# A two-layer flow backbone on one core: closings by groups of feature blocks, and layer 0's conditioning in products of 512 columns

## The chip, the cores and the metric

One core of a Trainium2 chip (trn2) runs the kernel once per launch. The metric is the device time of one execution in microseconds; a smaller number is better. The times shown are medians of several executions, and one execution more is profiled.

## What is computed

Two token groups pass through the same two layers: 128 context tokens and 256 latent (sample) tokens of 2048 features, 384 tokens in all. Each group has one conditioning vector, from which a layer makes six modulation vectors (shift, scale and gate, twice). In the reference, cut to what matters here:

```python
def trunk_layer(x, cvec, ctx_kv, lp):
    mods = jnp.split(jax.nn.silu(cvec) @ lp['w_ada'] + lp['b_ada'], 6, axis=-1)   # w_ada: 2048 x 12288
    sh1, sc1, g1, sh2, sc2, g2 = [m[:, None, :] for m in mods]
    h = rms_norm(x, lp['g_pre1']) * (1.0 + sc1) + sh1
    z = h @ lp['w_in']                                    # 2048 x 3072: q, k, v, pool, conv
    ...                                                   # attn (16 heads), pool, conv
    mix = jnp.concatenate([attn, pool, conv], axis=-1) @ lp['w_out']
    x = x + g1 * rms_norm(mix, lp['g_post1'])
    h = rms_norm(x, lp['g_pre2']) * (1.0 + sc2) + sh2
    f = jnp.square(jax.nn.relu(h @ lp['w_mlp1'])) @ lp['w_mlp2']   # 2048 x 8192 x 2048
    x = x + g2 * rms_norm(f, lp['g_post2'])
    return x, kv_out
```

All of it is float32.

## The kernel before

**Weights.** They stream from memory once, in loads of 512 KB into four slots (`raw`). ACT makes a high part of each load (`w_high`, L602), VectorE the low part that is left (`w_low`, L902), and TensorE multiplies three times (high by high, high by low, low by high) with the same split of the activations (`h_hi`, `h_lo`). Such a load is a *unit*; four units are a *quad*. `unit` (L1482) has 24 products of 384 columns; `unit_all` and `unit_tok` (L1491) keep the tokens still and stream 512 weight columns. ACT makes unit n + 4's high part when TensorE has used unit n, and SP loads a slot when its low part is made, so the four units ahead of TensorE are split and up to four behind those are loaded.

**Order.** Every engine's program is written out by hand, with semaphores between them. SP issues all streaming loads in one order. Layer 0 begins with eight 512-column blocks of `w_ada` that bring the first shift and scale. Then, in each layer: projections in pairs of blocks (`two_blocks`, eight units each); the attention loop (`step`, 24 steps: scores, softmax, turn, mix) with the first half of the output projection in pieces between (`side_piece`); the second half of the output projection and a *closing*; the MLP in eight chunks of eight quads; and again a closing, but for the last layer.

**Layer 0's conditioning.** The other 24 blocks of 256 columns of layer 0's `w_ada` (the gate of the first part, shift and scale of the second) run beside the projections (10 blocks) and the attention loop (14). A block is four quads of products in the four column groups of TensorE (`ada_unit`, L1565), each for one load of 512 rows by 256 columns. Its four partial rows are copied out by VectorE (`ada_copy`, L907), turned and added by TensorE (`ada_turn`, L1574), and added to the bias by VectorE (`ada_mods`, L911). A block's first product waits for the mods of the block before it.

**The later conditioning.** Layer 0's last gate and layer 1's blocks, 28 of 512 columns, are multiplied by VectorE during the MLPs (`products`, L933), up to three blocks in a chunk, two quads each. Such a block is folded by a transpose (L938) and a reduction (L942) into spare columns of `cond`, and TensorE turns it (`turn_sums`, L1616, four small products). That is done for each block, in the quads 2, 5 and 7. One late block runs in layer 1's projections.

**A closing** (`close_stage` on PE, ACT and VectorE, then `turn_x`). The last quarter of the output is added and gated for each token tile (tile 0 context, tiles 1 and 2 sample), its squares are summed, a Sqrt on ACT (`root_f`, L658) and a reciprocal give the norm, and x is updated (`update_x`, L1003). The squares of the new x give the next norm as a diagonal (`norm_x`, L1021). `turn_x` (L1546) multiplies 16 blocks of x of a tile by the diagonal, which turns and scales them at once. Then scale and shift are applied from PSUM (`modulate`: ACT L677, VectorE L1028, each four times 128 columns), and the result is split (`norm_high` L684; low parts by POOL, L510, for tiles 0 and 1 and by VectorE, L1036, for tile 2). The tiles go one after another, and fillers (`keep_warm`, L1535) stand after a tile's turns. Behind the last low part POOL zeroes the MLP's accumulator (L593), for which VectorE waits ahead of its MLP loop. The first unit of the next stage needs feature group 0 of all tiles (`h_wait`).

Of the kernel before, what the change touches and what calls it, by code (L numbers as in the profile page):

```python
# [31 lines left out]
F32 = mybir.dt.float32  # L32
# [5 lines left out]
P = 128  # L38
# [35 lines left out]
MODS_END = (ADA_BLOCKS, ADA_BLOCKS + ADA_WIDE)  # L74
# [6 lines left out]
WIDE_TURNS = (2, 5, 7)  # L81
WIDE_BLOCKS = ({0: ((0, 20, 1), (1, 0, 2), (1, 1, 2)), 4: ((1, 8, 3), (1, 9, 3), (1, 10, 3))},
# [8 lines left out]
def turn_of_quad(layer, lo, blocks=3):  # L91

    return {WIDE_TURNS[s]: s for s in range(min(blocks, len(WIDE_BLOCKS[layer][lo])))}

# [17 lines left out]
ADA_FIRST = (7, 6)  # L112
X_BANKS = (4, 5)
PAIRS = 8
ADA_FIRST_BLOCKS = 8
# [3 lines left out]
TURN_BANKS = ((4, 5, 6, 3), (0, 1, 2, 4), (5, 6, 3, 4))  # L119
TURN_FREED = ((None, None, None, None), (None, None, None, (0, 0)), ((0, 1), (0, 2), (0, 3), (1, 3)))  # L120
FILL = (0, 1, 5)
# [11 lines left out]
ADA_STEPS = 3 * (ADA_BLOCKS - ADA_MIX) // 2  # L133

# [34 lines left out]
def backbone(nc, x_prompt, x_sample, cache_k, cache_v, c, c_ctx, w_ada, b_ada, g_pre1, g_post1, g_pre2,  # L169
# [3 lines left out]
    with ctx:  # L173
# [44 lines left out]
        cond = new("cond", [DT, 32])  # L218
        folded = cond[:, :, 2:4].rearrange("p n g -> p g n")
# [4 lines left out]
        ada_s = at("ada_s", [UC], F32, sums_at + 4 * TOK)  # L224
# [6 lines left out]
        sinks = new("sinks", [DEPTH, HEADS])  # L231
# [49 lines left out]
        inv_x = at("inv_x", [TT], F32, stats_at + 288)  # L281

# [19 lines left out]
        xt_ready, full_act, full_dve, norm_hi, norm_lo, early_lo = sems("xt_ready full_act full_dve norm_hi norm_lo early_lo")  # L302
# [39 lines left out]

        block = ctx.enter_context(nc.Block())
# [3 lines left out]
        def _(sp):  # L347
# [35 lines left out]
            def load_blocks(layer, w, q, col, ada):  # L383

                for j in range(8):
                    load_unit(j, q, part(w, layer, 512 * (j % 4), col + UC * (j // 4)))
                    if ada is not None:
                        load_ada(ada[0], ada[1] + j // 4, j % 4)
# [20 lines left out]
            for layer in range(DEPTH):  # L409
# [20 lines left out]
                def load_pair(i, half, j, m):  # L430

                    for k in range(4):
                        load_ada(0, m, k)
                    load_out(i, half, j)
                    for k in range(2):
                        load_ada(0, m + 1, k)
                    load_out(i, half, j + 1)
                    for k in range(2, 4):
                        load_ada(0, m + 1, k)
# [49 lines left out]
        def _(pool):  # L489
# [3 lines left out]
            nc.gpsimd.memset(cond[:, :, :], 0.0).then_inc(consts_ready, 1)  # L493
# [9 lines left out]
            def early_lows(p):  # L503

                for t in range(2):
                    for g in range(4):
                        kts = slice(4 * g, 4 * g + 4)
                        pool.wait_ge(gate_done, 12 * p)
                        pool.wait_ge(norm_hi, 12 * (p - 1) + 4 * t + g + 1)
                        nc.gpsimd.tensor_tensor(h_lo[:, kts, tokens(t)], full[:, kts, tokens(t)], h_hi[:, kts, tokens(t)].bitcast(F32),  # L510
                                                ALU.subtract).then_inc(early_lo, 1)

            for layer in range(DEPTH):
                if layer == 0:
                    pool.wait_ge(h_ready, 8)
                else:
                    early_lows(2 * layer)
                    pool.wait_ge(early_lo, 8 * 2 * layer)
# [71 lines left out]
                early_lows(2 * layer + 1)  # L590
                pool.wait_ge(early_lo, 8 * (2 * layer + 1))
# [5 lines left out]
        def _(act):  # L597
# [74 lines left out]
            def modulate(p, t, g, layer, k, shift):  # L672

                act.wait_ge(xt_ready, 12 * (p - 1) + 4 * t + g + 1)
                for i in range(4):
                    kt = 4 * g + i
# [1277 lines left out]
```

## Time and profile before

| | us |
|---|---|
| median of 3 runs | 3249.17 |
| lowest and highest | 3248.01, 3249.87 |
| the profiled execution, whole | 3251.47 |
| its span, from the first to the last instruction | 3249.7 |
| TensorE busy in it | 3157.3 (97%) |
| VectorE, ACT, POOL busy | 2151.5, 1111.1, 215.8 |
| mean granted clock of TensorE | 0.99 of full |

The page gives busy time by engine, a chain of work that ended last, and groups of instructions by line. Busy shares are means over stages with different limits, so the stages are read one by one: with the table of stretches and the order of time. A float32 product stands as two records.

### The profile page before, as it was taken

To read this page: it belongs to the slowest core of one execution; us is meant where nothing else is said; L and a number is where in the kernel's file an instruction comes from. 1 tells how busy PE (TensorE), PEld (TensorE's weight loads), DVE (VectorE), ACT (ScalarE), POOL (GpSimd) and SP (SyncE) were. 2 spreads that over 40 slices of the span, in tenths; PEclk is the share of its full clock that TensorE was granted. 3 is DMA by queue.
4 is the path that set the end of the run, shared out by engine and by line. 5 is a ranking of instruction groups with operands and counts; after the bars stand their busy time and mean duration, and the time that the engine had idled before them with its cause. 6 is when DMAs were issued, how large, how long until landed. Compare 5 with 4: busy or idle time off the path is not lost.

```text
span 3249.7 us, 46901 instructions
## 1 busy us (share of the span) xinstructions
PE 3157.3 (97%) x16999; PEld 2733.6 (84%) x16999; DVE 2151.5 (66%) x3087; ACT 1111.1 (34%) x1531; POOL 215.8 (7%) x235
## 2 busy tenths in 40 slices
PE   7999999999999999999999999999999999999999
PEld 2688656798898998989988996679989899898997
DVE  2366665698988989889876888666646553334335
ACT  2222333533332333323334334353333233332333
POOL 0020132200000000000001303320000000000000
PEclk9999999999999999999999999999999999999999
DMA  9865575367676666767664331234545544444443
GB/s 350 285 208 185 164 233 175 128 218 228 217 222 217 225 218 208 229 212 237 208 213 134 111 124 61 95 119 156 175 132 178 167 138 128 130 126 126 129 124 142
DMA packets 404975, 574.75 MB, mean 177 GB/s; under 512 B 17881, under 2 KB 243921, under 8 KB 403441
## 3 DMA queue, kind: packets, MB, share of 16 engines
q1 hardware_dynamic: 401216, 560.02, 53.3%
q10 hardware_dynamic: 2288, 8.78, 0.7%
q0 software_dynamic: 1344, 4.33, 0.4%
q8 instruction: 72, 1.18, 0.1%
q14 instruction: 55, 0.44, 0.0%
HBM read 569.32 MB, written 3.74 MB: 176 GB/s over the span
## 4 chain that ended last, share of the span: by engine, by line
PE 86%; DVE 6%; issue 3%; ACT 2%; DMA 2%; SPq 0%; DVEq 0%; ACTq 0%
PE ps L1482 42%; PE ps L1491 35%; PE ps L1565 2%; DMA ada_raw<-in_w_ada_dram 1%; DVE w_lo L902 1%; DVE ada_sums L933 1%; PE ps L1588 1%; PE ps L1659 1%; PE ps L1750 1%; DVE conv L1191 1%; PE ps L1776 1%; PE ps L1764 1%; PE ps L1737 1%; ACT full L677 1%; DVE x L1003 1%
## 5 line engine op out<-in xcount | busy, mean ns | idle before, releaser
L902 DVE TENSOR_TENSOR w_lo<-raw,w_hi 128x1024 fp32r<-128x1024 f32 x660 | 810.0, 1232 | 737.2 <-ACT w_hi L602 716.1
L602 ACT ACTIVATE w_hi<-raw 128x1024 fp32r<-128x1024 f32 x660 | 697.8, 1059 | 1454.5 <-PE ps L1491 757.8
L1482 PE MATMUL ps<-h_hi,w_hi 128*128 128x384 f32 x2752 | 929.0, 338 | 4.9 <-DVE h_lo L1036 3.9
L1482 PE MATMUL ps<-h_hi,w_lo 128*128 128x384 f32 x2752 | 922.2, 335 | 0.0
L1482 PE MATMUL ps<-h_lo,w_hi 128*128 128x384 f32 x2752 | 921.9, 335 | 0.0
L1491 PE MATMUL ps<-w_hi,hid_hi 128*128 128x512 f32 x1500 | 586.0, 391 | 2.6 <-DVE facc L1404 2.6
L1491 PE MATMUL ps<-w_hi,hid_lo 128*128 128x512 f32 x1500 | 584.0, 389 | 0.0
L1491 PE MATMUL ps<-w_lo,hid_hi 128*128 128x512 f32 x1500 | 584.0, 389 | 0.0
L933 DVE SCALAR_TENSOR_TENSOR ada_sums<-ada_raw,cond,ada_sums 128x512 f32<-128x512 f32 x840 | 574.8, 744 | 0.0
L1482 PEld LDWEIGHTS ps<-h_hi,w_hi 128*128 128x128 f32 x2752 | 518.5, 188 | 21.2 <-issue 18.5
L1482 PEld LDWEIGHTS ps<-h_lo,w_hi 128*128 128x128 f32 x2752 | 518.4, 188 | 1.1
L1482 PEld LDWEIGHTS ps<-h_hi,w_lo 128*128 128x128 f32 x2752 | 518.2, 188 | 0.0
L1491 PEld LDWEIGHTS ps<-w_hi,hid_hi 128*128 128x128 f32 x1500 | 281.6, 188 | 63.3 <-DVE facc L1404 5.5
L1491 PEld LDWEIGHTS ps<-w_lo,hid_hi 128*128 128x128 f32 x1500 | 281.6, 188 | 58.6
L1491 PEld LDWEIGHTS ps<-w_hi,hid_lo 128*128 128x128 f32 x1500 | 281.6, 188 | 57.5
L1491 PE MATMUL ps<-w_hi,h_hi 128*128 128x512 f32 x348 | 149.0, 428 | 0.0
L1191 DVE SCALAR_TENSOR_TENSOR conv<-glu,pc,conv 128x384 f32<-128x384 f32 x240 | 141.8, 652 | 0.0
L1491 PE MATMUL ps<-w_lo,h_hi 128*128 128x512 f32 x348 | 138.4, 398 | 0.0
L1491 PE MATMUL ps<-w_hi,h_lo 128*128 128x512 f32 x348 | 138.4, 398 | 0.0
L1404 DVE TENSOR_TENSOR facc<-facc,ps 128x512 f32<-128x512 f32 x168 | 115.0, 685 | 30.4 <-PE ps L1491 28.5
L858 ACT ACTIVATE z<-ps 128x768 f32<-128x768 f32 x64 | 52.2, 815 | 202.8 <-PE ps L1482 202.8
L510 POOL TENSOR_TENSOR h_lo<-full,h_hi 128x512 fp32r<-128x512 f32 x24 | 34.3, 1466 | 1211.6 <-ACT h_hi L684 1211.6
(226 smaller groups left out, 2176.9 us busy)
## 6 DMA issues: line engine op xcount, KB each, us to landing
raw<-in_w_mlp_dram SPq DMA_DIRECT2D x512, 512.0 KB, 3.9
ada_raw<-in_w_ada_dram SPq DMA_DIRECT2D x360, 512.0 KB, 4.6
raw<-in_w_in_dram SPq DMA_DIRECT2D x96, 512.0 KB, 4.8
raw<-in_w_out_dram SPq DMA_DIRECT2D x64, 512.0 KB, 3.7
ada_aside<-in_w_ada_dram SPq DMA_DIRECT2D x24, 512.0 KB, 10.5
out_dram<-x SPq DMA_DIRECT2D x6, 512.0 KB, 2.6
x<-in_x_sample_dram SPq DMA_DIRECT2D x1, 2048.0 KB, 9.9
pw_w<-in_w_conv_pw_dram POOLq DMA_DIRECT2D x2, 1024.0 KB, 7.0
```

What stands on the lines that cost most here:

```text
L510: nc.gpsimd.tensor_tensor(h_lo[:, kts, tokens(t)], full[:, kts, tokens(t)], h_hi[:, kts, tokens(t)].bitcast(F32), ALU.subtract).then_inc(e ...
L602: nc.scalar.activation(dst[:, j % 4, :, :], raw[:, j % 4, :, :], ACT.Copy).then_inc(hi_ready, 1)
L677: last = nc.scalar.activation(full[:, kt, tokens(t)], ps[:, TURN_BANKS[t][g], P * i:P * i + P], ACT.Identity, scale=coef[:, k, kt, group(t ...
L858: nc.scalar.activation(z[:, 16:18, :], ps[:, 2 * pair:2 * pair + 2, 0:TOK], ACT.Relu).then_inc(acc_free, 1)
L902: nc.vector.tensor_tensor(low[:, j % 4, :, :], raw[:, j % 4, :, :], high[:, j % 4, :, :].bitcast(F32), ALU.subtract).then_inc(lo_ready, 1)
L933: op = nc.vector.scalar_tensor_tensor(out=out, in0=src, scalar=by, in1=out, op0=ALU.mult, op1=ALU.add)
L1003: nc.vector.scalar_tensor_tensor(out=res, in0=src, scalar=inv_f[:, t:t + 1], in1=res, op0=ALU.mult, op1=ALU.add).then_inc(x_updated, 1)
L1191: op = nc.vector.scalar_tensor_tensor(out=out, in0=src, scalar=w, in1=out, op0=ALU.mult, op1=ALU.add)
L1404: nc.vector.tensor_tensor(dst, dst, ps[:, BANK_ACC + t, :], ALU.add).then_inc(acc_added, 1)
L1482: last = nc.tensor.matmul(ps[:, 2 * pair + t, 0:TOK], w[:, j % 4, k, P * t:P * t + P], v[:, kt + k, :], start=begin and k == 0 and i == 0, ...
L1491: last = nc.tensor.matmul(ps[:, bank + t, :], v[:, kt + k, tokens(t)], wide(w, j)[:, k, :], start=begin and k == 0 and i == 0, stop=end an ...
L1565: last = nc.tensor.matmul(ps[32 * g:32 * g + 32, BANK_ADA, 0:UC], cond[:, 4 * j + g, :], ada_raw[:, j, g, :], start=j == 0, stop=j == 3)
```

## The change

- **Conditioning of layer 0.** The 24 blocks of 256 columns become 12 of 512, loaded as 256 rows by 512 columns. `ada_pair` multiplies two loads in one go, four products of 512 columns in the four column groups, behind every second unit and at four places in three attention steps. The blocks aren't turned one by one: `cond_at(kt, slot)` shifts the two vectors inside the 32 stationary columns, so that each block of a batch adds into rows of its own of the same bank, over a margin of zeros. There are two batches, of four and of eight blocks; each has one `batch_copy`, one `batch_turn` and one `batch_mods`. TensorE's loop over three pairs of projection blocks is written out in layer 0.
- **Closings.** The context tile is turned first. Then the sample tiles stand side by side in PSUM, and groups of four feature blocks are turned, modulated in 256 columns, split and freed one after another; POOL makes the context's low parts only, VectorE the sample's. ACT runs one Sqrt on a constant ahead of the closing (`root_seed`), and modulates a first context group before the last tile's squares. The fillers are one and four.
- **Turns of block sums.** `turn_sums` runs once for each chunk of an MLP, for its one to three blocks together.
- The sinks are kept once, with their sign changed.

```diff
-            def load_ada(layer, m, j):
-                sp.wait_ge(ada_used, 4 * m + j - 3)
-                src = w_ada[layer, 512 * j:512 * j + 512, bass.ds(m * UC, UC)]
-                sp.dma_start(ada_raw[:, j, :, :], src.rearrange("(k p) n -> p k n", p=P)).then_inc(ada_landed[j], 16)
+            def load_ada(layer, m, half, j):
+                sp.wait_ge(ada_used, 4 * m + (4 * half + j - 3))
+                row = 4 * 2 * P * half + 2 * P * j
+                src = w_ada[layer, row:row + 2 * P, bass.ds(m * UC, NC)]
+                sp.dma_start(wide(ada_raw, j), src.rearrange("(k p) n -> p k n", p=P)).then_inc(ada_landed[j], 16)
...
+            def ada_pair(w, v):
+                batch = 0 if w < BATCHES[1][0] else 1
+                first, n = BATCHES[batch]
+                begin, end = w == first and v == 0, w == first + n - 1 and v == 3
+                for u in (2 * v, 2 * v + 1):
+                    pe.wait_ge(ada_landed[u % 4], 16 * (2 * w + u // 4 + 1 - ADA_ASIDE))
...
+                for u in (2 * v, 2 * v + 1):
+                    for k in range(2):
+                        g = 2 * (u % 2) + k
+                        last = nc.tensor.matmul(ps[32 * g:32 * g + 32, BANK_ADA, :], cond_at(2 * u + k, w - first),
+                                                wide(ada_raw, u)[:, k, :], start=begin, stop=end)
+                    last.then_inc(ada_used, 1)
...
-                    if ada is not None:
-                        ada_beside(ada, j)
+                    if ada is not None and j % 2:
+                        ada_pair(ada, j // 2)
...
             def turn_x(p):
-                for t in range(TT):
-                    for g in range(4):
-                        pe.wait_ge(xn_ready, 3 * (p - 1) + t + 1)
...
+                pe.wait_ge(xn_ready, 3 * (p - 1) + 1)
+                for g in range(4):
+                    for i in range(4):
+                        last = turn_block(0, 4 * g + i, CTX_BANKS[g], P * i)
+                    last.then_inc(xt_ready, 1)
...
+                keep_warm(FILL[0], BANK_ADA)
+                pe.wait_ge(xn_ready, 3 * (p - 1) + 2)
+                turn_lat(1, 0)
+                keep_warm(FILL[1], BANK_ADA)
+                pe.wait_ge(xn_ready, 3 * (p - 1) + 3)
+                turn_lat(2, 0).then_inc(xt_ready, 1)
+                for g in range(1, 4):
+                    if g > 1:
+                        pe.wait_ge(full_act, ctx_full(p, 2 * g - 4))
+                        pe.wait_ge(full_dve, ctx_full(p, 2 * g - 3))
+                    turn_lat(1, g)
+                    turn_lat(2, g).then_inc(xt_ready, 1)
...
             def close_stage(r, before, layer, k, shift, q):          # VectorE
...
-                modulate(p, 0, 1, layer, k, shift)
+                modulate_ctx(p, 1, *how)
                 sum_squares_x(r, 2)
-                modulate(p, 0, 3, layer, k, shift)
                 norm_x(p, 2)
-                modulate(p, 1, 1, layer, k, shift)
-                modulate(p, 1, 3, layer, k, shift)
+                modulate_ctx(p, 3, *how)
+                modulate_lat(p, 0, *how)
+                low_lat(p, 0)
+                modulate_lat(p, 1, *how)
                 w_low(3, q)
-                modulate(p, 2, 1, layer, k, shift)
-                norm_low(p, 2, 0)
-                modulate(p, 2, 3, layer, k, shift)
-                for g in range(1, 4):
-                    norm_low(p, 2, g)
+                low_lat(p, 1)
+                for g in (2, 3):
+                    modulate_lat(p, g, *how)
+                    low_lat(p, g)
...
             def close_stage(r, q, layer, k, shift):                  # ACT
...
+                nc.scalar.activation(root_seed[:, :], ones[:, 0:1], ACT.Sqrt)
                 square_f(r, 3, 0)
                 root_f(r, 0)
...
-                        if k in turns and j == 2:
-                            turn_sums(wide_before(layer, lo, i, turns[k]))
+                        if k == turn_quad(layer, lo, blocks) and j == 2:
+                            turn_sums(wide_before(layer, lo, i, 0), blocks_of_chunk(layer, lo, blocks))
```

## Rows read from the trace of the kernel before

**Rows 1.** The page: TensorE's busy time, its share of the span, and its instructions.

```profile
PE 3157.3 (97%) x16999; PEld 2733.6 (84%) x16999; DVE 2151.5 (66%) x3087; ACT 1111.1 (34%) x1531; POOL 215.8 (7%) x235
```

**Rows 2.** Table of stretches: length, PE, PEld, DVE, ACT, POOL busy (count), clock, DMA, GB/s.

```profile
137.70:380.80 243.10, 231.35 (x1412) 197.57 (x1412) 156.88 (x236) 66.16 (x71) 26.83 (x41) 0.98 0.55 177
380.80:533.00 152.20, 148.29 (x1123) 90.12 (x1124) 89.05 (x223) 49.97 (x153) 45.99 (x40) 0.98 0.74 235
1732.50:1799.30 66.80, 66.78 (x384) 66.51 (x384) 42.07 (x53) 20.02 (x23) 4.13 (x8) 1.00 0.53 163
1732.50:1967.10 234.60, 227.66 (x1252) 217.51 (x1252) 188.33 (x265) 76.14 (x84) 34.18 (x52) 0.99 0.41 126
1967.10:2074.50 107.40, 103.89 (x619) 72.71 (x620) 82.56 (x195) 49.53 (x153) 45.86 (x40) 1.00 0.20 64
```

**Rows 3.** Order of time, layer 1's late turn: start, length, what, [idle before it, releaser].

```profile
1802.78 0.25 PE L1616 MATMUL ps<-cond,fold 128*32 128x8 f32 x8 [3.43 <-DVE cond L942]
```

**Rows 4.** Groups of PE by line: busy, mean ns of a record, idle before, releaser.

```profile
L1565 PE MATMUL ps<-ada_raw,cond 128*32 128x256 f32 x768 | 59.9, 394 | 7.9 <-DVE mods L911 7.9
L1574 PE MATMUL ps<-fold,ada_s 128*128 128x2 f32 x96 | 13.2, 242 | 7.8 <-DVE ada_s L907 7.8
```

**Rows 5.** Order of time, PE: two quads after a unit, then one quad.

```profile
141.77 0.34 PE L1482 MATMUL ps<-h_hi,w_lo 128*128 128x384 f32 x1
142.04 1.07 PE L1565 MATMUL ps<-ada_raw,cond 128*32 128x256 f32 x16
...
143.32 0.34 PE L1482 MATMUL ps<-h_lo,w_hi 128*128 128x384 f32 x1
...
147.14 0.34 PE L1482 MATMUL ps<-h_hi,w_lo 128*128 128x384 f32 x1
...
148.26 0.34 PE L1482 MATMUL ps<-h_lo,w_hi 128*128 128x384 f32 x1
```

**Rows 6.** DMA: size and median us to landing; attention loop of layer 0, then start.

```profile
ada_raw<-in_w_ada_dram SPq DMA_DIRECT2D x50, 512.0 KB, 4.9
raw<-in_w_out_dram SPq DMA_DIRECT2D x16, 512.0 KB, 6.3
...
ada_raw<-in_w_ada_dram SPq DMA_DIRECT2D x18, 512.0 KB, 10.0
```

**Rows 7.** Order of time: layer 0's closing behind attention, to VectorE's first MLP unit.

```profile
611.12 1.28 ACT L658 ACT_TABLE_LOAD   x1
612.65 0.16 DVE L998 RECIPROCAL inv_f<-std_f 128x1 f32<-128x1 f32 x1 [1.17 <-ACT std_f L658]
618.34 3.73 PE L1546 MATMUL ps<-diag,x 128*128 128x128 f32 x32
625.28 0.74 DVE L1003 SCALAR_TENSOR_TENSOR x<-gated,inv_f,x 128x512 f32<-128x512 f32 x1
625.95 1.36 DVE L1028 TENSOR_SCALAR full<-ps,coef,mods 128x128 f32<-128x128 f32 x4
628.97 0.29 DVE L1021 TENSOR_SCALAR diag<-ident,inv_x 128x128 f32<-128x128 f32 x1
641.03 0.43 PE L1482 MATMUL ps<-h_hi,w_hi 128*128 128x384 f32 x1 [0.76 <-DVE h_lo L1036]
650.53 1.23 DVE L902 TENSOR_TENSOR w_lo<-raw,w_hi 128x1024 fp32r<-128x1024 f32 x1 [5.63 <-POOL facc L593]
```

**Rows 8.** Order of time, VectorE in the first MLP chunk: one unit's four products.

```profile
658.71 2.73 DVE L933 SCALAR_TENSOR_TENSOR ada_sums<-ada_raw,cond,ada_sums 128x512 f32<-128x512 f32 x4
```

**Rows 9.** Table of stretches (columns as rows 2): first low parts of both MLPs.

```profile
650.50:719.90 69.40, 69.40 (x391) 67.07 (x391) 68.16 (x89) 26.82 (x29) 0.00 (x0) 1.00 0.67 212
2192.10:2228.70 36.60, 36.60 (x213) 36.60 (x212) 34.06 (x44) 14.37 (x15) 0.00 (x0) 1.00 0.56 173
```

**Rows 10.** Order of time, PE: the products around one turn of block sums.

```profile
686.72 0.34 PE L1482 MATMUL ps<-h_hi,w_lo 128*128 128x384 f32 x1
...
687.45 0.34 PE L1482 MATMUL ps<-h_lo,w_hi 128*128 128x384 f32 x1
```

More of the change, by code:

```diff
@@ L133 @@
 ADA_STEPS = 3 * (ADA_BLOCKS - ADA_MIX) // 2
+ROW_CHUNKS = (256, 384, 512, 896)
 def taps_at(u):
@@ L675, in modulate, with modulate_ctx @@
+            def modulate_ctx(p, g, *how):
+                act.wait_ge(xt_ready, ctx_turned(p, g))
                 for i in range(4):
-                    kt = 4 * g + i
-                    last = nc.scalar.activation(full[:, kt, tokens(t)], ps[:, TURN_BANKS[t][g], P * i:P * i + P], ACT.Identity,
-                                                scale=coef[:, k, kt, group(t):group(t) + 1],
-                                                bias=mods[:, layer, shift + kt, group(t):group(t) + 1])
+                    last = modulate(4 * g + i, 0, CTX, ps[:, CTX_BANKS[g], P * i:P * i + P], *how)
@@ L966, in eight_units @@
                         f()
-            def ada_pair(layer, m):
-                n = layer * ADA_BLOCKS + m
-                return ({3: [lambda: ada_copy(n)], 4: [lambda: ada_mods(layer, m, n)], 7: [lambda: ada_copy(n + 1)]},
-                        {7: [lambda: ada_mods(layer, m + 1, n + 1)]})
             def add_f(r, n, t, before):
@@ L1199, in _ @@
                 for i in range(3):
-                    before, after = ada_pair(0, i * 2 + ADA_QKV) if first else ({}, {})
-                    for j in range(8):
-                        after[j] = [lambda c=c: tap(c) for c in taps_at(8 * i + j)] + list(after.get(j, []))
-                    eight_units(quad(layer, Q_IN + 4) + i * 2, before, after)
+                    after = {j: [lambda c=c: tap(c) for c in taps_at(8 * i + j)] for j in range(8)}
+                    eight_units(quad(layer, Q_IN + 4) + i * 2, None, after)
                 def pool_means():
@@ L1341, in _ @@
                     what = i % 3
-                    m = ADA_MIX + 2 * (i // 3)
-                    if first and what == 0 and 0 < i <= ADA_STEPS:
-                        ada_mods(0, m - 1, m - 1)
-                    if first and what == 1 and i < ADA_STEPS:
-                        ada_copy(m)
                     if i >= 4:
@@ L1576, in ada_turn, with batch_turn @@
+            def batch_turn(batch):
+                n = BATCHES[batch][1]
+                pe.wait_ge(ada_copied, 2 * ADA_FIRST_BLOCKS + batch + 1)
+                for t in range(4):
+                    last = nc.tensor.matmul(ps[:, BATCH_BANKS[batch], 2 * n * t:2 * n * t + 2 * n],
+                                            sums_flat[:, ROW_CHUNKS[t]:ROW_CHUNKS[t] + P], fold[:, 0:2 * n], start=True, stop=True)
                 last.then_inc(ada_turned, 1)
@@ L1816, in step @@
                         if ada and what == 0:
-                            ada_unit(m, 3)
-                        if ada and what == 1:
-                            ada_unit(m + 1, 0)
-                        if ada and what == 2:
-                            ada_turn(m + 1)
+                            ada_pair(w, 1)
                     if i >= 3:
```

358 lines of the change are left out of this document (193 added, 165 removed).

## Prediction

> **What bounds the kernel now.** The page comes first: TensorE is busy for 3157.3 of 3249.7 us [rows 1], so a gain has to come from work taken off TensorE's queue or from the 92 us in which it stands. The table of stretches shows where the two layers differ, and that is the yardstick here: layer 1 runs the same projections and the same attention loop as layer 0, without layer 0's conditioning products between them [rows 2]. Attention with its side units takes 152.2 us in layer 0 and 107.4 us in layer 1. The stretch from the first whole pair of projection blocks to the first scores takes 243.1 us with 40 units in layer 0, and 234.6 us with 48 units in layer 1. Sixteen undisturbed units take 66.8 us, so one takes 4.175 us and one of its 24 products 0.174 us. Layer 1's 234.6 us hold one late block turn, which stood 3.43 us [rows 3] and costs 0.4 us itself.
>
> **Layer 0's conditioning.** 24 blocks of 256 columns become 12 of 512. Before, TensorE turns aside once for each quad of `ada_unit` (four products in four column groups) and once for each `ada_turn`; the groups by line give 768 and 96 records, and 7.9 us of waiting for VectorE's `ada_mods` and 7.8 us for its `ada_copy` [rows 4]. The price of one aside comes from the order of time: from the last product before a single quad to the second product after it are 1.12 us, two product steps (0.35 us) of which would have passed anyway, so it costs 0.77 us; two quads in one place cost 1.55 - 0.35 = 1.20 us [rows 5]. So a quad streams for 0.43 us, and turning aside costs 0.34 us. Twice the columns make 0.86 us for a quad of 512 columns; the streaming stays the same in sum, and the asides halve.
>
> Projections: layer 1's 234.6 us less the late turn (3.8) and eight units (33.4) leave 197.4 us as the bare stretch; layer 0 pays 45.7 us on top for ten blocks. After the change these are five wide blocks, 20 asides of 0.86 + 0.34 us, 24.0 us, and one batch turn of four small products, not in the trace: 0.4 us if it is like a turn of block sums (below), 1.2 if its full-width weights count three times; I take 0.8, nearer to the former. Together 24.8 us. **Gain 20.9 us.** Layer 1's stretch contains its own waits for VectorE's tail (layer norm, pooling); if layer 0 meets less of them, up to 2 us more.
>
> Attention: 152.2 - 107.4 = 44.8 us for 14 blocks. 56 quads stream 24.1 us, 14 turns at 0.38 us make 5.3 us, and the granted clock of 0.98 on 152 us costs 3.0 us; what is left is 12.4 us, 0.22 us for each aside (some of them stand where TensorE changes operands anyway). After: 28 asides of 0.86 + 0.22, 30.2 us, and 0.8 us for the second batch turn. With 0.34 us an aside it would be 34.4 us. Gain 10.4 to 13.8 us, from which I take 1.4 us for a DMA wait (next paragraph): **12.4 us.** The waits for VectorE's copies and mods [rows 4] are inside both differences; the batch's own copy stands in VectorE's queue ahead of a low part, with three units ready for TensorE behind it, so it hides.
>
> What is moved is the wait on the loads. `ada_pair` needs two loads at once and frees two at once, and SP, which issues in order, holds the weight loads behind the conditioning loads: in the projections four of eight weight loads are now issued four units ahead of their use instead of five or six. Three units are 13 us; a load lands in 4.9 to 6.3 us in the busiest stretch [rows 6], and the splits into high and low parts take ACT and VectorE some 2.3 us; so it stays covered by 4 us, and that is what goes first if the loads slow down. In the attention loop the third pair of a block is loaded when the first is used, a step and a pair before (107.4 / 24 + 1.1 = 5.6 us), where a load's median is 4.9 to 6.3 us. Between nothing and 0.7 us for each of seven blocks, I take 0.2, as a pair is only of the 4.9 us kind.
>
> **The closings** (three). TensorE's part runs from the end of VectorE's residual update U to the first unit of the next stage: U = 625.28 + 0.74 = 626.0 and the unit at 641.0, 15.0 us [rows 7]; the same pair of rows stands in all three closings, 15.0 us each. Behind U, before: two modulations (1.36 us each) and the norm, so the third diagonal at U + 3.2; 16 turns, five fillers, the tail of ACT's modulations and splits. After: one modulation and the square of the last tile on ACT, diagonal at about U + 2.7; then 28 turns at 3.73 / 16 = 0.233 us without a wait, to U + 9.4. The first unit needs only feature group 0, whose split I have done at U + 7.5. That chain is turn, two 256-column modulations, a 1024-column split on ACT and one on VectorE; the modulation is not in the trace, it lies between one and two of 128 columns (0.34 to 0.68 us), and I take 0.48, nearer to one since an operation of 512 columns takes 2.73 / 4 = 0.68 us [rows 8] and not four times 0.34; the ends move the unit by nothing, since TensorE's turns end last. So the unit starts at U + 9.5, **5.5 us earlier, three times**. ACT and VectorE go on with groups 1 to 3 until about U + 20, one unit ahead of TensorE.
>
> The early Sqrt takes a function-table load out of the chain in the two closings behind attention. The load is 1.28 us, and VectorE waited 1.17 us for the root [rows 7]; from the load's end to the reciprocal are 0.25 us, which stay with a handover, 0.3 in all: 0.87 us each, 1.7 us for both. The Trainium skill, page "ScalarE: Activation LUTs", section "What ACT_TABLE_LOAD costs", counts a drain of 1.38 us on top of a load of 1.283 us. The trace agrees on the load; the square root ran right behind it, so no row shows that drain. By the skill's figures it would be an estimated 5.3 us for two and the time 3.6 us lower.
>
> Not all of it stays. VectorE starts the MLP's low parts only when POOL has zeroed the accumulator, at 650.5 us [rows 7], and that clock hardly moves, since the zeroing waits for the last low part. TensorE stood 6 us behind VectorE there; with a start at 634.7 its unit 4 is due at 651.4 and VectorE has it at 651.7. From there VectorE needs 68.2 us of work for 16 units in layer 0, and 34.1 us for eight in layer 1, whose products end there [rows 9]; TensorE needs 66.4 (the last four units have 18 products of 512 columns, some 4.1 us) and 33.4. With the 0.3 us that is **2.0 us back** in layer 0 and, counted in the same way, **0.8 us back** in layer 1. The middle closing leads into projections with few products and keeps all. Closings: 16.5 + 1.7 - 2.8 = **15.4 us**.
>
> **Turns of block sums in the MLP.** 28 become 13 (23 in layer 0 become 8). One costs 0.73 - 0.35 = 0.38 us [rows 10]; fifteen are 5.7 us. 24 columns instead of 8 in eight of them return some 0.4 us: **5.3 us**. The last turn of each chunk stays where it was, so its wait doesn't change; two more small `block_mods` at the end of a chunk fall into VectorE's idle quad.
>
> The merged sinks, the zeroed margin of the conditioning vectors and SP's wider rows cost nothing: they lie at the start beside loads, or change no count.
>
> **Sum:** 20.9 + 12.4 + 15.4 + 5.3 = 54.0 us. The profiled execution took 3251.5 us (span 3249.7 and 1.8 around it), so 3197.5; it lies 2.3 us over the median of the three runs, so the forecast is **3195 us**. Bounds: projections 16 to 23, attention 6 to 17, closings 8 to 19, turns 4 to 6.
>
> **Rivals.**
> (a) VectorE takes the closings back: if the tail of a closing on ACT and VectorE is 3 us longer than I have it, the MLP starts 3 us later in both layers and unit 1 waits too; the closings keep 5 us and the time is 3205. For it: VectorE is the only engine with work in that hole, and 650.5 is a wait for POOL. Against it: VectorE's own work there stays some 11 us (28 instructions become 20), and POOL has four low parts left instead of eight.
> (b) The loads become the wait: with pairs freed at once the mean landing grows to 8 us; the third and fourth pair of each attention block wait some 1.5 us each and three of eight weight units 0.5 us, 27 us in all: 3222. For it: that loop already has DMA at 0.74 [rows 2], and a shorter loop raises it to 0.82. Against it: rows are 2 KB instead of 1 KB, and no wait for this load shows before.
> (c) The four column groups don't run side by side at 512 columns: a quad would cost 1.72 us, 48 times 0.86 us more: 3236. Against it: two 256-column quads in one place add 0.43 us, what four groups side by side make.
> (d) Slower. The attention loop becomes bound by the latency of its pairs: TensorE stands at each of its 28 pairs, with the softmax chain behind it on the same queue. It decides at 54 / 28 = 1.9 us a pair; at 2.5 us the time is 3265. For that a load would have to land in 8 us and more on all pairs; it took 10.0 us where the queues were full in the start [rows 6], but here 4.9.
>
> **How the numbers follow.** Forecast 0.74, (a) 0.11, (b) 0.09, (c) 0.03, (d) 0.03. The forecast's own bounds give 3184 to 3215 with all terms at one end, which is unlikely; the range 3182 to 3214 takes in (a) and a quarter of (b), and 2 us below for the spread of the runs shown. 0.2% is 6.5 us, about what a measurement of this kernel can tell from no change. The forecast, (a), (b) and (c) are all faster, 0.97; of (d) I put 0.01 within 0.2% (1.9 us a pair) and 0.02 beyond it.
>
> **What would show it.** In the profile after: records of the conditioning products in the same stretches at half the count and some 0.6 us each, quads of 1.0 us; no idle time of TensorE in front of them on VectorE; 222 and 138 us for the two stretches of layer 0; first unit 9 to 10 us behind U in each closing, and no table load in the chain; then waits for `w_lo` in the first MLP chunk of layer 0, some 2 us; 104 records of block sums, eight a turn [rows 3], instead of 224. It is wrong if TensorE waits for `ada_raw`, if weight units wait for ACT's high parts in the projections, or if the first chunk of the MLP ends at the time at which it ended before.

## The result and the profile after

| | before | after |
|---|---|---|
| median, us | 3249.5 | 3217.5 |
| profiled execution, us | 3251.5 | 3218.1 |
| its span, us | 3249.7 | 3215.7 |
| ratio to before | | 0.990 [0.989, 0.991] |

The change makes the kernel 32 us faster; the forecast was 54 us, 3195 us, with a range that ended at 3214. The page of after, to be held against [rows 1]:

```profile
span 3215.7 us, 45526 instructions
...
PE 3126.3 (97%) x16409; PEld 2707.3 (84%) x16409; DVE 2149.1 (67%) x3021; ACT 1104.2 (34%) x1498; POOL 204.6 (6%) x223
```

TensorE's busy time fell by 31.0 us. The table of stretches shows where the forecast's 54 us came and where they did not. Columns as in [rows 2]; in order of time: layer 0's projections, its attention loop, the first closing from the first turn to the first unit, the first MLP chunk, the second chunk; the middle closing, which leads into layer 1; then the last closing and the first chunk of layer 1's MLP.

```profile
138.04:368.38 230.34, 220.73 (x1220) 188.57 (x1221) 153.94 (x219) 65.66 (x71) 30.75 (x41) 0.99 0.57 187
368.38:507.30 138.92, 135.68 (x847) 75.91 (x846) 84.58 (x197) 49.52 (x153) 45.92 (x40) 1.00 0.76 258
592.69:609.01 16.32, 15.19 (x107) 12.45 (x106) 13.61 (x32) 13.08 (x29) 2.98 (x2) 1.00 0.48 162
609.01:751.13 142.12, 136.34 (x683) 122.36 (x682) 123.45 (x156) 48.62 (x53) 8.72 (x3) 0.98 0.61 195
751.13:884.11 132.98, 132.69 (x682) 120.57 (x680) 118.19 (x153) 43.60 (x44) 0.00 (x0) 1.00 0.68 221
1682.06:1698.41 16.35, 15.20 (x108) 12.45 (x106) 13.63 (x32) 13.08 (x29) 2.99 (x2) 1.00 0.01 2
2126.63:2142.95 16.32, 15.20 (x108) 12.45 (x106) 13.61 (x32) 13.09 (x29) 2.98 (x2) 1.00 0.48 162
2142.95:2282.45 139.50, 134.60 (x683) 122.38 (x682) 78.69 (x89) 48.58 (x53) 8.72 (x3) 0.99 0.45 144
```

The closings and first chunks of the kernel before, in the same view and order (22.69 us of closing and 133.84 of chunk in layer 0, the middle closing 21.78, 22.69 and 133.79 in layer 1):

```profile
618.34:641.03 22.69, 18.17 (x110) 14.07 (x108) 16.43 (x43) 19.30 (x47) 9.33 (x7) 0.92 0.49 163
641.03:774.87 133.84, 133.47 (x696) 120.92 (x697) 120.01 (x157) 44.50 (x48) 7.37 (x3) 1.00 0.61 198
1710.74:1732.52 21.78, 18.15 (x110) 14.21 (x108) 15.52 (x43) 19.29 (x47) 9.29 (x7) 0.92 0.08 25
2159.96:2182.65 22.69, 16.50 (x109) 12.96 (x108) 16.34 (x43) 19.29 (x47) 9.32 (x7) 0.99 0.50 163
2182.65:2316.44 133.79, 133.79 (x680) 122.27 (x681) 75.09 (x88) 44.47 (x48) 7.36 (x3) 0.99 0.45 142
```

By stretch, in us gained (the spans differ by 34.0; the measured column adds up to that but for rounding):

| stretch | forecast | measured |
|---|---|---|
| projections of layer 0 | 20.9 | 12.8 |
| attention loop of layer 0 | 12.4 | 13.3 |
| three closings, first turn to first unit | 18.2 | 6.4 + 5.4 + 6.4 = 18.2 |
| what the first MLP chunks give back | -2.8 | -9.1 - 5.7 = -14.8 |
| turns of block sums | 5.3 | 0.8 + 4.9 = 5.7 |
| the start, and layer 1's projections and attention | 0 | -0.3 - 2.0 + 1.2 = -1.1 |

(The first chunk of layer 0 is 8.3 us longer and saves 0.8 of turns like every chunk there; so it gives back 9.1.) Two rows are wrong: 12 us in the first chunks and 8 us in the projections.

**The first MLP chunk.** Order of time in layer 0: the start, the length, what, and in brackets the idle time before it and its releaser. First VectorE, then TensorE, then one stretch of the table with the granted clock third from the end:

```profile
626.09 1.23 DVE L959 TENSOR_TENSOR w_lo<-raw,w_hi 128x1024 fp32r<-128x1024 f32 x1 [5.62 <-POOL facc L632]
...
694.42 3.48 DVE L959 TENSOR_TENSOR w_lo<-raw,w_hi 128x1024 fp32r<-128x1024 f32 x3
697.82 2.12 DVE L1466 TENSOR_TENSOR facc<-facc,ps 128x512 f32<-128x512 f32 x3
```

```profile
698.56 0.79 PE L1553 MATMUL ps<-w_hi,hid_hi 128*128 128x512 f32 x1 [3.69 <-DVE facc L1466]
699.15 0.63 PE L1553 MATMUL ps<-w_hi,hid_lo 128*128 128x512 f32 x1
699.58 0.63 PE L1553 MATMUL ps<-w_lo,hid_hi 128*128 128x512 f32 x1
...
704.34 0.39 PE L1553 MATMUL ps<-w_lo,hid_hi 128*128 128x512 f32 x1
704.57 0.39 PE L1553 MATMUL ps<-w_hi,hid_hi 128*128 128x512 f32 x1
```

```profile
698.56:703.56 5.00, 5.00 (x12) 3.94 (x13) 2.49 (x3) 0.00 (x0) 0.00 (x0) 0.50 0.97 338
```

VectorE begins the MLP at 626.09 us, as in [rows 7] held up by POOL's zeroing, and comes to its first add at 697.82 without a pause. TensorE stands 3.69 us for that add. Then the granted clock is 0.50 for 5 us (1.2 of 2.4 GHz): twelve products step by 0.43 us, where they step by 0.23 at 704 us, 2.6 us more. In layer 1 the same lag shows at the turn of block sums (behind this hole the granted clock is 0.66 on the mean of 5 us):

```profile
2194.45 0.25 PE L1692 MATMUL ps<-cond_all,fold 128*32 128x8 f32 x8 [3.75 <-DVE cond_all L1005]
```

**The projections.** Here TensorE stands twice, 4.08 us for the batch's copy and 3.66 us for the conv taps that the sums of the layer norm need. SP, ACT and VectorE ahead of the first, VectorE ahead of the second, then both products:

```profile
290.89 0.37 SPq L405 DMA_DIRECT2D ada_raw<-in_w_ada_dram  x1
291.44 1.13 SPq L391 DMA_DIRECT2D raw<-in_w_in_dram  x1
```

```profile
297.57 1.06 ACT L641 ACTIVATE w_hi<-raw 128x1024 fp32r<-128x1024 f32 x1 [5.95 <-DMA raw<-in_w_in_dram]
```

```profile
298.67 1.23 DVE L959 TENSOR_TENSOR w_lo<-raw,w_hi 128x1024 fp32r<-128x1024 f32 x1 [3.66 <-ACT w_hi L641]
299.81 2.73 DVE L1258 SCALAR_TENSOR_TENSOR conv<-glu,pc,conv 128x384 f32<-128x384 f32 x5
...
302.92 0.28 DVE L968 COPY sums_flat<-ps 128x128 f32<-128x128 f32 x1
...
311.27 1.23 DVE L959 TENSOR_TENSOR w_lo<-raw,w_hi 128x1024 fp32r<-128x1024 f32 x1 [4.29 <-ACT w_hi L641]
312.41 2.20 DVE L1258 SCALAR_TENSOR_TENSOR conv<-glu,pc,conv 128x384 f32<-128x384 f32 x4
```

```profile
303.35 1.07 PE L1650 MATMUL ps<-ada_raw,cond_all 128*32 128x512 f32 x8 [4.08 <-DVE sums_flat L968]
314.80 4.51 PE L1780 MATMUL ps<-conv,ones 128*128 128x384 f32 x8 [3.66 <-DVE small L1264]
```

SP issues the weight load only behind the conditioning load whose slot comes free with the pair at 290.7 us; it lands 6 us later; ACT's high part, the low part, five taps and only then the copy follow. The second hole has the same shape: a low part that waits 4.29 us for its high part, and four taps behind it. How the waiting is shared between the two holes changes from execution to execution: in three other runs that leave the projections as they are (the old closings, the moved wait and the run without zeroing below) they are 3.9 and 4.1, 2.7 and 4.7, and 2.6 and 4.8 us, 7.4 to 8.0 together.

### The profile page after: what moved, and what is told of

It is laid out like the page before. It is cut to its first block, busy times and chain, and to the rows that moved or that the text cites. A ratio compares the mean times of both kernels' runs of the same rounds, so it can differ in the third digit from the quotient of the medians.

```text
span 3215.7 us, 45526 instructions
## 1 busy us (share of the span) xinstructions
PE 3126.3 (97%) x16409; PEld 2707.3 (84%) x16409; DVE 2149.1 (67%) x3021; ACT 1104.2 (34%) x1498; POOL 204.6 (6%) x223
## 4 chain that ended last, share of the span: by engine, by line
PE 82%; DVE 8%; issue 5%; DMA 3%; ACT 2%; POOL 0%; SPq 0%; DVEq 0%; ACTq 0%; POOLq 0%
PE ps L1544 40%; PE ps L1553 35%; DVE ada_sums L996 2%; DMA ada_raw<-in_w_ada_dram 2%; DVE w_lo L959 1%; PE ps L1650 1%; PE ps L1673 1%; PE ps L1735 1%; PE ps L1861 1%; PE ps L1849 1%; PE ps L1835 1%; PE ps L1822 1%; DVE x L1061 1%; DMA raw<-in_w_in_dram 0%; ACT w_hi L641 0%
## 5 line engine op out<-in xcount | busy, mean ns | idle before, releaser
L996 DVE SCALAR_TENSOR_TENSOR ada_sums<-ada_raw,cond_all,ada_sums 128x512 f32<-128x512 f32 x840 | 575.1, 745 | 0.0
L1553 PEld LDWEIGHTS ps<-w_hi,hid_hi 128*128 128x128 f32 x1500 | 282.2, 188 | 68.2 <-DVE facc L1466 10.3
L549 POOL TENSOR_TENSOR h_lo<-full,h_hi 128x512 fp32r<-128x512 f32 x12 | 19.4, 1618 | 1225.6 <-ACT h_hi L732 1225.6
```

The costliest lines, as they stand in the source:

```text
L996: op = nc.vector.scalar_tensor_tensor(out=out, in0=src, scalar=by, in1=out, op0=ALU.mult, op1=ALU.add)
L1553: last = nc.tensor.matmul(ps[:, bank + t, :], v[:, kt + k, tokens(t)], wide(w, j)[:, k, :], start=begin and k == 0 and i == 0, stop=end an ...
```

## Experiments

Each run stood beside the kernel before on its own chip (3249.2 to 3250.7 us there). The times are medians of four to ten executions, which lie 3.2 to 7.3 us apart in one kernel (3213.5 to 3218.4 for the changed one), so a difference of two or three microseconds between two kernels is not clear of that spread.

**Old closings.** The changed kernel with `close_stage`, `turn_x`, the low parts and the fillers of before:

```diff
-LAT_BANKS = ((0, 1), (2, 7), (4, 5), (6, 3))
-FILL = (1, 4)
+TURN_BANKS = ((4, 5, 6, 3), (0, 1, 2, 4), (5, 6, 3, 4))
+FILL = (0, 1, 5)
...
```

> The changed kernel with the closings of before (tiles one after another, POOL's low parts for two tiles, no early square root, fillers 0, 1 and 5); conditioning in 512 columns and one turn of block sums for a chunk stay. It measures what the closings are worth by themselves. Theory V: the closings ahead of the two MLPs give nothing, only the middle one keeps its 5 us less some of it later, so 1 to 5 us are lost: 3219 to 3222. The prediction's own account, closings worth 15.4 us: 3233.

Measured: 3220.0 us. So the closings are worth 2.5 us, which the spread does not tell from nothing, and not 15.4. Its two first chunks, without a hole:

```profile
613.28:747.95 134.67, 134.37 (x680) 122.22 (x681) 118.80 (x155) 43.51 (x45) 6.11 (x2) 0.99 0.62 197
2150.32:2282.69 132.37, 132.37 (x680) 120.85 (x681) 75.13 (x88) 44.47 (x48) 7.37 (x3) 1.00 0.45 144
```

**The wait for the zeroing moved**, in the changed kernel and in the one before:

```diff
-                dve.wait_ge(facc_zero, layer + 1)
                 for lo, hi in PARTS:
...
                         for k in range(Q_CHUNK):
+                            if k == 4:
+                                dve.wait_ge(facc_zero, layer + 1)
```

> The changed kernel with one wait moved: VectorE waits for POOL's zeroing of the accumulator at the MLP's fifth quad, where it first adds into it, and no longer ahead of the MLP. Theory V (VectorE's start is the bound of both first MLP chunks, and took the closings' gain back): in the changed kernel VectorE stands 5.62 us there (626.09 us, layer 0), then works without a pause to the end of its first adds, 73.9 us later; TensorE waits for it in pieces of 0.5 to 0.6 us and in one of 3.69 us at 694.87 us, and its products run at 0.43 us a step instead of 0.23 for the next 5 us. With a start 5.6 us earlier the long hole goes in both layers, with its slow stretch: the first chunk of layer 0 falls from 142.1 us to 133.5 to 135, that of layer 1 from 139.5 to 133 to 134, and the whole by 12 to 14 us, to some 3204. Rival L (the loads or ACT's high parts are late behind the closing, and VectorE only waits beside them): VectorE starts earlier but meets late high parts, the holes stay above 2 us, and the whole falls by less than 4 us.

> The kernel before with the same wait moved. Theory V: there VectorE was just in time. TensorE's second half of the first chunk in layer 0 needs the accumulator's bank at about 724.5 us and VectorE's first add ends at 724.0; in layer 1 the first chunk is 1.5 us over a later one. So the earlier start is worth nothing in layer 0 and at most 1.5 us in layer 1: 3247 to 3250. Rival M (the wait costs much in either kernel, and has nothing to do with the new closings): it falls by some 13 us as the changed kernel does, to 3237.

Measured: 3213.1 and 3249.1 us. The first is a miss: 4 us at most (3211.9 to 3218.5 us, against 3213.5 to 3218.4 for the changed kernel), near the rival's time, but not for its reason. The hole of 3.7 us in layer 0 stayed, and that in layer 1 was 3.0. VectorE began at once, behind its last low part, with its high parts there; then its second operation stuck. VectorE and POOL in layer 0:

```profile
623.50 1.22 DVE L959 TENSOR_TENSOR w_lo<-raw,w_hi 128x1024 fp32r<-128x1024 f32 x1
624.64 4.98 DVE L994 TENSOR_SCALAR ada_sums<-ada_raw,cond_all 128x512 f32<-128x512 f32 x2
```

```profile
623.71 5.25 POOL L632 MEMSET facc<- 128x6144 f32 x1 [2.29 <-DVE h_lo L1103]
```

Two `TENSOR_SCALAR` that take 0.88 us elsewhere took 4.98, until POOL's memset was over (628.96); in layer 1 it was 4.97. The low part just before ran beside the memset at its usual 1.22. The Trainium skill, page "SBUF — State Buffer", section "Who interferes with whom", has a port pair that VectorE and GpSimd share under an exclusive lock: `tensor_scalar` may need it, and an operation with two inputs in SBUF meets only a GpSimd operation that reads SBUF. Both rows agree. So the wait was not what had to go, but the memset. The run on the kernel before tells less than it was meant to, since the memset held VectorE there as well (two `TENSOR_SCALAR` took 3.14 us); the run after the next stands in for it, with the old closings in the changed kernel.

**No zeroing.** The first chunk's sums are copied into the accumulator, in an iteration ahead of VectorE's loop:

```diff
-                nc.gpsimd.memset(facc[:, :, :, :], 0.0).then_inc(facc_zero, 1)
...
+                    if first_chunk:
+                        nc.vector.tensor_copy(dst, ps[:, BANK_ACC + t, :]).then_inc(acc_added, 1)
+                    else:
+                        nc.vector.tensor_tensor(dst, dst, ps[:, BANK_ACC + t, :], ALU.add).then_inc(acc_added, 1)
```

> The changed kernel without POOL's zeroing: the first chunk of each MLP copies its sums into the accumulator instead of adding them, in iterations written out ahead of VectorE's loop. In the run with the wait moved, VectorE began at once, but its second operation stood beside POOL's memset (623.71 to 628.96 us) and took 4.98 us for two instructions that take 0.88 us otherwise, so the earlier start was lost again; without the memset nothing holds it. Theory V (VectorE's start decides): its first low part of the MLP of layer 0 comes within 1.5 us of its last low part of the closing instead of 5.6, the hole of 3.69 us in layer 0 and that of 3.75 us in layer 1 shrink below 1 us, the first chunks take 133.5 to 135.5 and 132.3 to 133.5 us instead of 142.1 and 139.5, and the whole is 11 to 15 us under the changed kernel: 3202 to 3206. Rival L (late loads or high parts behind the closing): the holes stay above 2 us and the gain stays under 5 us.

Measured: 3202.3 us, 15 us under the changed kernel. Its closing's last low part, its MLP's first, and both first chunks:

```profile
618.64 1.23 DVE L1101 TENSOR_TENSOR h_lo<-full,h_hi 128x1024 fp32r<-128x1024 f32 x1 [1.19 <-ACT h_hi L735]
619.79 1.22 DVE L957 TENSOR_TENSOR w_lo<-raw,w_hi 128x1024 fp32r<-128x1024 f32 x1
620.92 0.88 DVE L992 TENSOR_SCALAR ada_sums<-ada_raw,cond_all 128x512 f32<-128x512 f32 x2
```

```profile
608.41:742.36 133.95, 132.98 (x684) 120.69 (x682) 123.56 (x156) 48.64 (x53) 3.49 (x2) 1.00 0.64 206
2133.82:2267.11 133.29, 132.66 (x683) 120.81 (x682) 78.77 (x89) 48.61 (x53) 3.48 (x2) 1.00 0.47 151
```

Counted from the first unit, VectorE starts 5.7 us earlier; the chunks are 1.0 us over the later ones (133.0 and 132.3) instead of 9.1 and 7.2. The rival with late loads falls.

**Old closings and no zeroing**, both edits together:

> The changed kernel with the closings of before and without POOL's zeroing. With the zeroing the closings are worth 2.5 us (3220.0 with the old ones, 3217.5 with the new). Theory V (they were worth what the prediction said, and VectorE, standing for the zeroing, took it back): the old closings gain little from an early VectorE, 0 to 3 us, as TensorE comes late there anyway (their first chunks take 134.7 and 132.4 us, 1.6 and 0.1 over a later one): 3217 to 3220, so that without the zeroing the new closings are worth 15 to 18 us against 3202.3. Rival Z (leaving out the zeroing is a gain of its own in either kind of closing, 10 us and more): 3206 to 3210, and the closings are worth 4 to 8 us.

Measured: 3218.2 us. With the old closings the zeroing costs 1.8 us, within the spread; with the new ones 15. Without it the new closings are worth 3218.2 - 3202.3 = 15.9 us, against a forecast of 15.4. So the closings' term as a whole was sized rightly, to within the spread, and was taken back by one thing that the sum had left standing.

**The batch's copy one low part earlier:**

```diff
-                    eight_units(quad(layer, Q_IN + 4) + i * 2, None, after)
+                    eight_units(quad(layer, Q_IN + 4) + i * 2, {7: [lambda: batch_copy(0)]} if first and i == 2 else None, after)
...
-                before = {0: [lambda: batch_copy(0)], 3: [lambda: batch_mods(0)]} if first else {}
+                before = {3: [lambda: batch_mods(0)]} if first else {}
```

> The changed kernel with VectorE's copy of the first conditioning batch moved one low part forward in its queue: ahead of the low part for the fourth unit of the last projection pair instead of behind it and its five taps. Theory Q (queue order behind a late load): in the changed kernel the copy is done at 303.2 us because the low part in front of it waited 3.66 us for ACT, and ACT for a load that landed at 297.55; TensorE stood 4.08 us at 299.27 and ran at a lower clock for the next unit (5.7 instead of 4.2 us). The copy needs only the products that ended at 290.7, so it is done at 296 and the first hole goes. The second hole, at the sums for the layer norm (3.66 us at 311.14), hangs on the conv taps behind the next late low part and stays or grows, to 3.7 to 4.7 us. Whole: 4 to 6 us less, 3212. Rival P (TensorE's quad itself waits for its load, and the copy only ends at the same time): the hole stays, 3217.

Measured: 3213.6 us. The first hole is gone; the second grew, by more than expected:

```profile
298.55 1.07 PE L1650 MATMUL ps<-ada_raw,cond_all 128*32 128x512 f32 x8
...
310.10 2.29 PE L1780 MATMUL ps<-conv,ones 128*128 128x384 f32 x3 [5.30 <-DVE small L1264]
```

**And the taps ahead of the late low part:**

```diff
-                after = {j: [lambda c=c: tap(c) for c in taps_at(24 + j)] for j in range(8)}
+                after = {j: [lambda c=c: tap(c) for c in ([*taps_at(24), *taps_at(25), *taps_at(26)] if j == 0 else [])] for j in range(8)}
```

> The changed kernel with the batch's copy one low part earlier, as in the run before, and with the last nine conv taps of the last projection pair all ahead of the low part for its sixth unit instead of four of them behind it. Theory Q (both holes in layer 0's projections come from VectorE's queue behind low parts whose loads SP holds back): with the copy alone the first hole went and the second grew to 5.30 us, since the last four taps ended at 309.9 us behind a low part that came at 306.6. Ahead of it they end at some 304.9, when TensorE reaches the sums at 304.8; the second hole falls under 1 us, with the slow stretch behind it. Layer 1 has the same code and loses its 0.49 us there. Whole: 9 to 12 us under the changed kernel, 3206 to 3209. Rival T (the tail of layer norm and pooling behind it takes it back: TensorE stands longer at 350 us): 3211 to 3214.

Measured: 3210.9 us, at the edge of the rival's time; but the rival's place, TensorE at 340 us, has 1.87 us as in the changed kernel. The second hole fell to 1.79 us, not under 1, and the stretch to 224.5 us, so the gain was smaller for that reason.

**SP's order: two weights, then two conditioning loads:**

```diff
-                    if ada is not None:
-                        load_ada(ada[0], ada[1], j // 4, j % 4)
+                    if ada is not None and j % 2:
+                        for u in (j - 1, j):
+                            load_ada(ada[0], ada[1], u // 4, u % 4)
```

> The changed kernel with SP's order in layer 0's projections changed from weight, conditioning, weight, conditioning to two weights and then two conditioning loads. It takes away the wait of every second weight load behind a conditioning load whose slots come free only with a pair of quads. Theory D (SP's queue makes the weights late: in the changed kernel the load that landed at 297.55 us was issued at 291.44, 2.3 us after its slot's low part was made at 289.1): these loads are issued 1 to 2.3 us earlier, and the two holes fall from 7.7 us together to 3 to 5.5; whole 2 to 6 us less, 3211 to 3215. Rival E (loads follow the slots, not SP's order; or the conditioning then comes late and TensorE waits for it): the holes stay, 3216 to 3219.

Measured: 3207.6 us, better than theory D had it. SP's queue and the stretch:

```profile
280.99 1.00 SPq L405 DMA_DIRECT2D ada_raw<-in_w_ada_dram  x2
282.24 0.93 SPq L391 DMA_DIRECT2D raw<-in_w_in_dram  x2
290.54 1.77 SPq L405 DMA_DIRECT2D ada_raw<-in_w_ada_dram  x2
```

```profile
137.69:360.01 222.32, 218.87 (x1220) 187.13 (x1220) 154.16 (x219) 65.98 (x71) 29.63 (x41) 0.99 0.59 193
```

The weight that was issued at 291.44 us, behind the next pair's conditioning load, now goes out with the pair before, at 282 us: one weight load more stands ahead of every conditioning pair, a gain of a whole pair (9 us), not of 1 to 2.3. Without a change to VectorE's order the first hole is gone, the second is 2.65 us instead of 3.66 and the one at 340 us 0.8 instead of 1.9. So the late loads caused the first hole and a part of the second, and VectorE's order passed them on: with the loads as late as before, the copy moved forward took the first hole away too, and the taps moved forward brought the second to 1.79. The stretch is 222.3 us; the forecast was 222.2.

**The causes together:** no zeroing, copy and taps (first), and SP's order on top (second):

> The changed kernel without POOL's zeroing, with the batch's copy one low part earlier and with the taps ahead: the two causes taken away together. If both theories hold and the two don't overlap, the gains add up: 11 to 15 and 9 to 12 us, so 3191 to 3197, which is where the prediction had the change itself (3195, with 54 us of gain). If they overlap (the same wait counted twice), 3200 to 3206.

> All that helped, in one kernel: no zeroing, the copy one low part earlier, the taps ahead, and SP's order with two weights ahead of two conditioning loads. With the three first the stretch of layer 0's projections is 224.3 us, with a hole of 1.79 us at the sums for the layer norm and one of 1.85 at 340 us; with SP's order alone it is 222.3. If the order's gain goes on top (it makes VectorE's low parts early, so that the first hole goes and the second falls under 0.9, as in its own run): 220 to 222 us there and 3190 to 3193 in the whole. If it is the same wait that both take away: 3193 to 3195.

Measured: 3193.9 and 3188.0 us (the latter 0.981 [0.980, 0.982] of before). The first two gains add up: 15.2 for the zeroing and 6.6 for copy and taps, 21.8 us, and 23.7 measured. SP's order brings 5.8 us more on top, not the 9.9 that it brought alone, so a part of it is the same wait; even so the time is under the 3190 to 3193 us that was expected. (That text gives the second hole as under 0.9 us in the run of SP's order alone; the trace has 2.65 there, and 1.14 in this run.) The second kernel is the best here, 29.5 us under the changed one; its stretch of projections:

```profile
137.66:358.54 220.88, 218.94 (x1220) 187.11 (x1221) 154.06 (x219) 65.73 (x71) 29.61 (x41) 0.99 0.61 199
```

## Why the prediction was wrong

**The step that failed most: "Not all of it stays".** It counted 68.2 us of VectorE's work for 16 units and stopped there, at a give-back of 2.0 us. VectorE's queue doesn't stop there: three low parts and the first add follow, and TensorE needs that add 72 products after the first of its last four units. In the kernel before that meeting had hardly any slack. Its first add (three in this row) begins at 723.31 us, so it ends at 724.0, and TensorE comes to it at 708.08 + 72 x 0.2266 = 724.4:

```profile
723.31 2.12 DVE L1404 TENSOR_TENSOR facc<-facc,ps 128x512 f32<-128x512 f32 x3
```

The sum should have been this, counted from the first turn: TensorE 6.4 us earlier; VectorE's start 1.2 later (33.4 instead of 32.2 us); its work to the end of the first add 1.1 shorter (72.4 instead of 73.5); 0.4 of slack; 6.1 us that TensorE must stand. It stood 3.7 us there, and its 16 units took 2.3 us more than before, 6.0 together. The 2 us of waits for `w_lo` that the text foresaw are in these units (1.2 us of such waits in layer 0's chunk); the hole was not foreseen. Layer 1's 0.8 us failed in the same way, at the fold of the first block. Rival (a) also had VectorE take the closings back, but by a closing's tail 3 us longer than forecast. The tail grew by some 1 us only: the last low part ends at 620.5 us, U + 21.0, where the text had about U + 20. It too ended at the units. (Two small slips of the text's own sums: the give-backs come to 2.1 and 1.0 us instead of 2.0 and 0.8, and rival (b)'s waits to 28.5 instead of 27.)

**The clock behind a hole was left out.** The long holes cost more than their length here: 2.6 us more behind the one of 3.69. The kernel before shows it behind its late turn, the hole of [rows 3], where 3.8 us were taken for the whole; one microsecond of it in the table of stretches:

```profile
1803.70:1804.70 1.00, 1.00 (x5) 1.00 (x4) 0.85 (x3) 0.34 (x1) 0.56 (x2) 0.50 0.00 0
```

At 0.50 for some 3.4 us it lost 1.7 us more, so the bare stretch is 195.7 us rather than 197.4, and the projections should take 220.5. The best kernel takes 220.9.

**The batch's copy "hides": wrong.** It named the low part behind the copy and the three units that TensorE has ready, not the low part and five taps in front of it. The wait on the loads was seen and sized ("four units ahead instead of five or six"), and the units indeed never waited for it. What waited stands behind the low parts on VectorE: the copy and the taps. The holes cost 7.7 us and the slow products behind them some 3 more (the unit behind the first took 5.8 us instead of 4.3, the sums 4.1 instead of 2.4 in layer 1, from their start to the next product), 11 us where 8.1 of the forecast are missing; 1.7 of the difference is the bare stretch, the rest is not traced. Rival (b) had the loads, but at TensorE's products; waits for `ada_raw` came to 2.3 us in all:

```profile
L1650 PE MATMUL ps<-ada_raw,cond_all 128*32 128x512 f32 x384 | 51.1, 604 | 6.3 <-DVE sums_flat L968 4.1 <-DMA ada_raw<-in_w_ada_dram 2.3
L1692 PE MATMUL ps<-cond_all,fold 128*32 128x24 f32 (+2 forms) x104 | 3.4, 196 | 7.2 <-DVE cond_all L1005 7.2
```

**What was right.** The conditioning records are 384 at 0.60 us, half the count of [rows 4]. An aside, one quad of 512 columns, takes 1.20 us: the last product ahead of one starts at 146.29 and the second behind it at 147.84, less two steps; the price had been 0.86 + 0.34. Attention: 138.9 us where 138 to 140 was forecast. The closings to the first unit: U is 598.75 + 0.75 = 599.5 and the unit 609.0, U + 9.5 as written. VectorE waits 0.27 us for the first root instead of 1.17:

```profile
586.11 0.16 DVE L1056 RECIPROCAL inv_f<-std_f 128x1 f32<-128x1 f32 x1 [0.27 <-ACT std_f L697]
...
598.75 0.75 DVE L1061 SCALAR_TENSOR_TENSOR x<-gated,inv_f,x 128x512 f32<-128x512 f32 x1
...
601.52 1.16 DVE L1079 TENSOR_SCALAR diag<-ident,inv_x 128x128 f32<-128x128 f32 x1
```

```profile
601.34 1.26 POOL L549 TENSOR_TENSOR h_lo<-full,h_hi 128x512 fp32r<-128x512 f32 x1 [64.63 <-ACT h_hi L732]
```

That U + 9.5 came out to the digit is in part luck. The third diagonal was forecast for U + 2.7 and ends at U + 3.2, while the 28 turns behind it take 6.3 us and not the 6.7 that the text left for them. The diagonal is late because its `TENSOR_SCALAR`, 0.29 us in all nine places before, takes 1.16 to 1.19 us in each of the three closings and ends with POOL's first low part of the context, which stands beside it. TensorE waits for that diagonal, 1.13 us in layer 0. So some 0.9 us a closing (1.16 - 0.29, an estimate) may be left there; no run moves POOL's low part to show it.

The two closings that lost a table load gained 6.4 us and the one that had none 5.4, so by this difference the early Sqrt is worth 1.9 us in both together; no run takes it away by itself. The trace had said 1.7. The 5.3 us by the figures of the page "ScalarE: Activation LUTs" of the Trainium skill, section "What ACT_TABLE_LOAD costs", are not borne out on this path. The turns of block sums gave 5.7 us where 5.3 was forecast; their 104 records are there, but "its wait doesn't change" fell in layer 1's first chunk with the 3.75 us.

What stays open: layer 1's projections took 2.0 us more than before. 0.6 of it is a wait of the first unit; behind the same late turn of 3.43 us the granted clock stayed at 0.50 for some 6.1 us instead of 3.4, which loses 1.3 us more. Why one hole is followed by different lengths of half clock is open: no run here varies that by itself.

## What to carry to other kernels

When a stage is made to start earlier, follow every other engine's queue past the stage's first instructions to the next place where the engines meet, and write down the slack there: an engine whose start is fixed by something else (here a memset) can give back the gain at that place (here 6.0 of 6.4 us in layer 0, before the slow products). When a wait moves on a load queue, list what stands behind the consumer's wait on its own engine, not only the consumer of the data. And price a hole of TensorE with the slow products behind it, from a hole of the same trace, as a range: the same hole of 3.43 us lost 1.7 us more in one execution and 3.0 in another.

## What was not expected of the hardware

- POOL's memset of 6144 columns (5.25 us) stopped a VectorE `TENSOR_SCALAR` of 512 columns until its end (4.98 us for two, else 0.88), while a subtraction of two operands ran beside it at its usual 1.22 us.
- A VectorE `TENSOR_SCALAR` of 128 columns (0.29 us) took 1.16 to 1.19 us beside a POOL subtraction of 512 columns, in all three closings.
- A hole of 3.69 us on TensorE was followed by 5 us at a granted clock of 0.50, which cost 2.6 us more; behind one hole of 3.43 us, the same in two kernels, half clock lasted 3.4 us in one execution and 6.1 in the other.
